# Layers' attention: sparse chunks' output products first, scaling ahead of low parts, and two output pieces' low parts formed by VectorE

## The reference, cut to what matters

```python
...
        ret = head_groupnorm(ret, g_ret[l].reshape(RET_HEADS, RET_DV).astype(jnp.float32))
        o_c = (jax.nn.silu(rg.astype(jnp.float32)) * ret.reshape(B, S, RET_HEADS * RET_DV)).astype(x.dtype)

        x = x + jnp.concatenate([o_a, o_b, o_c], axis=-1) @ w_out[l]

        hf = rmsnorm(x, g_mlp[l])
        x = x + jnp.square(jax.nn.relu(hf @ w_ff1[l])) @ w_ff2[l]
```

## Time and profile before

| | us |
|---|---|
| three runs | 1396.71, 1397.04, 1401.29 |
| median | 1397.04 |
| the profiled execution's own time | 1395.43 |
| its span | 1393.4 |
| granted TensorE clock, mean | 0.998 of full |

### The profile page before, as it was taken

One profiled execution on the slowest core, in us unless ns is written; L12 is line 12 of the kernel. 1 busy time (PEld: TensorE's weight loads), 2 busy tenths in 40 slices (PEclk: granted clock), 3 DMA queues, 4 the chain that ended last, 5 costly groups with the idle time before them and its releaser, 6 DMA issues.

```text
span 1393.4 us, 19892 instructions
## 1 busy us (share of the span) xinstructions
PE 1347.1 (97%) x7754; PEld 931.0 (67%) x7754; DVE 622.7 (45%) x1060; ACT 541.0 (39%) x790; POOL 449.3 (32%) x295
## 2 busy tenths in 40 slices
PE   8998999999999999999999999999999999999998
PEld 7786788887887788888887877755434444344343
DVE  5685554544687455353344887523202112122021
ACT  6667644435576654343555562212111111111011
POOL 2384454444374544543867913000000000000000
PEclk9999999999999999999999999999999999999999
DMA  7441454553533355455786351479999999999997
GB/s 289 137 168 67 152 181 181 185 202 127 207 116 110 116 204 190 181 182 181 237 278 225 103 208 52 137 290 411 422 428 428 427 428 428 428 427 427 428 423 292
DMA packets 50250, 351.99 MB, mean 253 GB/s; under 512 B 7747, under 2 KB 9679, under 8 KB 25583
## 3 DMA queue, kind: packets, MB, share of 16 engines
q1 hardware_dynamic: 49438, 349.52, 64.9%
q10 hardware_dynamic: 720, 1.20, 0.2%
HBM read 347.78 MB, written 1.07 MB: 250 GB/s over the span
## 4 chain that ended last, share of the span: by engine, by line
PE 72%; DMA 11%; DVE 7%; ACT 3%; issue 3%; DVEq 2%; POOL 1%; SPq 0%; ACTq 0%; POOLq 0%
PE psum L1925 12%; PE psum L1101 9%; PE psum L1103 9%; PE psum L1102 9%; PE psum L1396 9%; DMA ring<-in_w_expert_up 8%; PE psum L1946 5%; PE psum L1398 4%; PE psum L1091 4%; PE psum L1853 2%; POOL weights_split L908 1%; PE psum L1863 1%; DMA arena<-in_w_expert_down 1%; DVE arena L2577 1%; ACT weights_split L2040 1%
## 5 line engine op out<-in xcount | busy, mean ns | idle before, releaser
L908 POOL TENSOR_TENSOR weights_split<-weights_raw,weights_split 128x512 fp32r<-128x512 f32 (+2 forms) x253 | 401.6, 1621 | 338.2 <-ACT weights_split L2040 338.2
L2040 ACT ACTIVATE weights_split<-weights_raw 128x2048 fp32r<-128x2048 f32 (+4 forms) x154 | 243.5, 1586 | 243.5 <-PE psum L1103 145.3
L1925 PE MATMUL psum<-ring,arena 128*64 128x512 f32 x944 | 226.5, 598 | 12.1 <-DMA ring<-in_w_expert_up 11.2
L1396 PE MATMUL psum<-h_split,weights_split 128*128 128x512 f32 x512 | 182.1, 399 | 3.1 <-DVE h_split L2028 2.7
L1925 PEld LDWEIGHTS psum<-ring,arena 128*64 128x64 f32 x944 | 73.4, 138 | 136.4 <-issue 135.8
L1101 PE MATMUL psum<-weights_split,h_split 128*128 128x512 f32 (+3 forms) x400 | 151.9, 380 | 4.3 <-POOL weights_split L908 2.4
L1101 PE MATMUL psum<-weights_split,hidden_split 128*128 128x512 f32 (+1 forms) x384 | 151.1, 393 | 4.3 <-DVE hidden_split L2028 4.3
L908 DVE TENSOR_TENSOR weights_split<-weights_raw,weights_split 128x2048 fp32r<-128x2048 f32 (+3 forms) x53 | 119.3, 2257 | 70.1 <-ACT weights_split L2040 68.3
L1102 PE MATMUL psum<-weights_split,h_split 128*128 128x512 f32 (+3 forms) x400 | 149.5, 374 | 0.0
L1103 PE MATMUL psum<-weights_split,h_split 128*128 128x512 f32 (+3 forms) x400 | 149.2, 373 | 0.0
L1103 PE MATMUL psum<-weights_split,hidden_split 128*128 128x512 f32 (+1 forms) x384 | 147.3, 384 | 0.0
(11 more groups left out here) (379 smaller groups left out, 1734.5 us busy)
## 6 DMA issues: line engine op xcount, KB each, us to landing
weights_raw<-in_layer_w SPq DMA_DIRECT2D x94, 1024.0 KB, 4.8
arena<-in_w_expert_down SPq DMA_DIRECT2D x28, 2048.0 KB, 14.7
ring<-in_w_expert_up SPq DMA_DIRECT2D x28, 2048.0 KB, 15.0
ring<-in_w_expert_gate SPq DMA_DIRECT2D x23, 2048.0 KB, 16.2
weights_raw<-in_second_w SPq DMA_DIRECT2D x44, 512.0 KB, 4.7
arena<-in_w_expert_gate SPq DMA_DIRECT2D x4, 2048.0 KB, 10.2
ring<-in_w_expert_up SPq DMA_DIRECT2D x8, 1024.0 KB, 13.1
arena<-in_w_expert_down SPq DMA_DIRECT2D x16, 512.0 KB, 12.3
```

The lines of the kernel that those rows point to most:

```text
L908: ins = eng.tensor_tensor(W.part(j, 1, n)[:, cols], W.raw(j, n)[:, cols], W.part(j, 0, n).bitcast(F32)[:, cols], ALU.subtract)
L1396: pe.matmul(both.rearrange("p (w s) -> p w s", w=2), w[0][:, k, f * P:(f + 1) * P], hTp[:, :, k, :], start=(k == 0), stop=False)
L1925: ins = pe.matmul(bank[half(j), :], xe[h][:, k, half(j)], w[j][:, k, :], start=(k == 0), stop=(k == KD - 1))
L2040: act.activation(W.part(j, 0, w), W.raw(j, w), ACT.Copy).then_inc(W.hi, 1)
```

## The change

Five edits, all in the first block's two layers, none in what is computed:

1. TensorE: the sparse chunks (0, 1) of piece (0,1) are multiplied for both token tiles ahead of retention's chunks (2, 3): six matmuls before `turn_retained`, six after it.
2. TensorE: half of `project_out(1, 0, 0)` moves ahead of `attend_values(7)`, the other half to the end, and all of `project_out(1, 0, 1)` comes after the first `tr3` transposes. The unit `wout` 2 is finished later, after `wout` 1.
3. VectorE: `low_values(0)` comes after the rotation; from group 6 on each `norm_probs(g)` comes before the low part that stood ahead of it; `add_out(2)` comes after `add_out(1)`.
4. VectorE instead of GpSimd forms the low parts of `("out", 1, 1)` and `("out", 0, 0)`: one instruction of 2048 columns each, ahead of `norm_probs(4)` and of `norm_probs(7)`.
5. ScalarE: the high copies of pieces (0,0) and (1,0) come one group later, and `exponentials(9)` before `empty_turned(8)`.

```diff
@@ layer_plan
-    plan += [wout[0], turned[8], values[7], wout[2], turned[9], values[8], values[9], wout[1]] + turned_x[:2] + [wout[3]] + turned_x[2:]
+    plan += [wout[0], turned[8], values[7], turned[9], values[8], values[9], wout[1], wout[2]] + turned_x[:2] + [wout[3]] + turned_x[2:]
@@ layer_pieces
-    p += [(("out", c, i), "P", None if i else ("wout", T * c + T - 1)) for i in (1, 0) for c in range(2)]
+    p += [(("out", c, i), "V" if c == i else "P", None if i else ("wout", T * c + T - 1)) for i in (1, 0) for c in range(2)]
@@ TensorE
                 attend_mla(5)
+                units.wait_emptied(("O", 0))
+                project_out(0, 1, 0, (0, 1))
                 ret_ready.wait(pe, 1, l)
                 turn_retained()
-                units.wait_emptied(("O", 0), ("mixT", 3))
-                project_out(0, 1, 0, range(4))
                 units.wait_emptied(("O", 2))
-                project_out(0, 1, 1, range(4), True)
+                project_out(0, 1, 1, (0, 1))
+                units.wait_emptied(("mixT", 3))
+                project_out(0, 1, 0, (2, 3))
+                project_out(0, 1, 1, (2, 3), True)
                 turn_probs(4)
@@ 
                 turn_probs(8)
+                project_out(1, 0, 0, (0, 1))
                 attend_values(7)
-                project_out(1, 0, 0, range(4))
                 turn_probs(9)
@@ 
                 project_out(0, 0, 1, (3,))
-                project_out(1, 0, 1, (0, 1))
+                project_out(1, 0, 0, (2, 3))
                 units.wait_emptied(("wout", 0), ("wout", 1))
                 transposes(pe, units, "tr3", x, (0, 1))
-                project_out(1, 0, 1, (2, 3))
+                project_out(1, 0, 1, range(4))
@@ ScalarE
                 empty_turned(4)
-                split_after("ukv", 0, 0)
                 empty_turned(5)
                 exponentials(6)
                 high_values(4)
-                split_after("out", 0, 1)
+                split_after("ukv", 0, 0)
                 empty_turned(6)
                 exponentials(7)
                 high_values(5)
+                split_after("out", 0, 1)
                 empty_turned(7)
                 exponentials(8)
                 high_values(6)
                 split_after("out", 1, 1)
+                exponentials(9)
                 empty_turned(8)
-                exponentials(9)
@@ VectorE
                 norm_probs(3)
-                low_values(0)
                 units.wait_emptied(*(("uq", j) for j in range(2 * T)))
                 rotate(dve, *halves(q[:, :, :, NOPE:QK]), *angles(ROPE), q_tmp).then_inc(q_roped.sem, 1)
+                low_values(0)
@@ 
+                split_low(LW, dve, LW.index["out", 1, 1], l)
                 norm_probs(4)
                 norm_probs(5)
                 mask_scores(6)
+                norm_probs(6)
                 low_values(4)
-                norm_probs(6)
                 mask_scores(7)
+                split_low(LW, dve, LW.index["out", 0, 0], l)
+                norm_probs(7)
                 low_values(5)
-                norm_probs(7)
                 mask_scores(8)
+                norm_probs(8)
                 low_values(6)
-                norm_probs(8)
                 mask_scores(9)
                 add_out(0)
+                norm_probs(9)
                 low_values(7)
-                norm_probs(9)
-                add_out(2)
                 low_values(8)
                 low_values(9)
                 add_out(1)
+                add_out(2)
```

## The result

| | before | changed |
|---|---|---|
| median of the runs | 1396.88 us (4 runs, 1396.60 to 1401.29) | 1388.05 us (4 runs, 1387.26 to 1389.19) |
| the profiled execution's own time | 1395.43 us | 1389.19 us |
| its span | 1393.4 us | 1387.4 us |

The ratio is 0.9931, with a 95% interval of 0.9910 to 0.9953: 8.8 us faster, 6.6 at the least by the interval (0.47% of 1396.88). The forecast was 1390.0, in a range of 1386.5 to 1394.0.

What follows compares the result with a forecast made beforehand. TensorE was taken as the bound, with only its idles in the layers' attention to win. 2.71 + 1.0 - 0.2 = 3.5 us a layer, 7.0 in two, takes the median 1397.04 to 1390.0 us; range 1386.5 to 1394.0.

Steps and rivals of the forecast that it cites:

- The bound and what could be won: Feed-forward and expert stretches untouched; only TensorE's six idles per layer, 6.24 us, 12.5 in two layers, can be won.
- The rotation: Ahead of the transposed queries: rotation before low_values(0) starts TensorE 0.74 us earlier; 0.6 of the idle stays.
- Sparse chunks first: At retention's turn: 2.17 us idle shrinks to about 0.6; 2.15 us earlier in all by the next transpose.
- only idles count: TensorE's accounting: matmuls are the same before and after, so only idle times matter to the gain.
- VectorE's first low part: Piece (1,1) ahead of norm_probs(4): costs at most 0.35 us; total gain shrinks to 1.51 us after group 5.
- The scaling of group 6: Ahead of group 6's transpose: later copy and earlier scaling remove the whole 1.20 us; 2.71 us earlier in all.
- VectorE's second low part: Piece (0,0) ahead of group 7's scaling: in time, costs nothing; without cover 2.28 us at most.
- GpSimd and (1,0): Ahead of attend_values(7): GpSimd's remaining piece is the tightest place; 0.2 us a layer taken as loss.
- GpSimd and VectorE get in each other's way: Rival, chance 0.17: beside groups 8 and 9's scalings, 1.5 us lost a layer instead of 0.2; 1392.6 us.
- The feed-forward entry: Before ff1: twelve matmuls cover the 0.94, 0.19 grows to about 0.65, 0.41 nears 0; 1.0 us earlier.
- The sum: Whole layer: 2.71 + 1.0 - 0.2 = 3.5 us gained, 7.0 us in two layers, reaching the end.
- the contention: The 0.2 us a layer deducted for GpSimd's piece (1,0) possibly being late ahead of attend_values(7).

Runs made afterwards that it cites:

- r1: Kernel before with only low_values(0) moved behind VectorE's rotation; profiled execution 1399.76 us.
- r2: Kernel before with only TensorE's sparse chunks of piece (0,1) first for both token tiles; profiled execution 1392.46 us.
- r6: Changed kernel with ScalarE's copies of (0,0) and (1,0) back one group earlier; profiled execution 1388.57 us.
- r10: Changed kernel with low_values(4) ahead of the scaling of group 6 again; profiled execution 1387.92 us.
- r3: Changed kernel with the low parts of output pieces (1,1) and (0,0) back on GpSimd; profiled execution 1394.36 us.
- r5: Changed kernel with GpSimd's low parts in steps of 256 columns, not 512; profiled execution 1385.68 us.
- r7: Changed kernel with its second edit undone, wout 2 and add_out(2) back too; profiled execution 1387.91 us.
- r4: The changed kernel unaltered, run again beside the kernel before; median 1388.15 us against 1396.83, ratio 0.9938.
- r8: Changed kernel with ff1's first two low parts exchanged: (0,0) by VectorE, (0,1) by GpSimd; median 1385.51 us against 1396.61, ratio 0.9913.

## Why the prediction was right, and where its steps were not

**The bound and what could be won.** Right. Only idles of the attention and at the feed-forward's entry went, and the feed-forward is full in both. The expert stretch did not lengthen by what was won: from the first product on the gathered rows (L1853, L1856 after) to the end of the span it took 441.0 us in both profiles of before and 441.8 and 441.0 in those of the change. The 543 us of the rows do not show this, for they are the width of the window in both.

**The rotation.** Forecast 0.74, measured 1.0 (r1). I added the 0.42 us of `low_values(0)` to an end of 108.8 for the rotation; but VectorE's instructions follow each other 0.34 apart, not 0.42 (108.46, 108.80), the rotation began at 106.46, and TensorE started 0.05 after the end. The start is 0.14 us earlier than my 106.4 (this execution is 0.20 behind), and with the two small overlaps that makes the 0.26 us, to a few hundredths.

**Sparse chunks first.** The idle was right: 0.51 against the forecast 0.6, and retention's high part at 117.77 against 117.93. That "only idles count" was not: alone the edit took 1.76 us of idle and gave 1.2 (r2).

**VectorE's first low part.** Right in its working, and nearly in size: 119.50 to 121.78 against 119.74 to 121.94 forecast. The idle at group 4 did not show, that at group 5 was 0.23 against 0.3, from the exponentials as said. At group 6 the gain by starting times was 2.96 (132.39 to 129.43), with the changed execution 0.20 behind at the start of the stretch (107.71 and 107.91), so 3.16 against the forecast 2.71. The bracketed idles alone, 4.70 to 1.07, say 3.63: my rule that only idles count leaves out that the broken-up groups keep TensorE busy for 20.34 us and not 19.98, and a gap of 0.11 that has no bracket.

**The scaling of group 6.** Right: the whole 1.20 went. I had named two reasons, and r6 and r10 show that one of them would do. That the scaling itself would be back at 0.69 us, because GpSimd is idle beside it, I had left open ("if it again lasts 1.0 longer"); it is a third reason that no run separates.

**VectorE's second low part.** Right: hidden, its scaling at 133.7 where 133.8 was forecast. What it gained, and the first piece with it, is 0.35 us in two layers (r3).

**GpSimd and (1,0).** I took 0.2 us for a delay of the piece (1,0). That term was put in the wrong place and was too small. The piece was in time (TensorE went on at 139.60 without idle). The scaling of group 9 was not: 1.83 us, and 0.86 of idle. This is the mechanism of the rival "GpSimd and VectorE get in each other's way", at the second of its two places, and twice as large there as its 0.4. r5 shows its cause: with GpSimd's instructions half as long, the excess fell from 1.14 to 0.49. The pair of 0.69 and "1.62 and 1.72" that I had set down for the rival was a selection: the kernel before also has scalings of 0.69 (group 7, at 135.88) and 0.79 us (group 9, at 145.36) while GpSimd was at work. The rule that I set beside it (the Trainium skill, page "SBUF — State Buffer", section "SBUF: two separate sides": an exclusive lock held for the whole instruction) agrees with this, and the other direction shows too: GpSimd's piece took 7.48 us in r6, and in the kernel before its instruction at 135.92 took 1.78 us. I had priced the rule as if each meeting were TensorE's loss; the one at group 8 (1.56 us) cost TensorE nothing, since there was cover.

**The feed-forward entry, 1.0 us.** This step failed as a gain of the second edit: 1.0 us forecast, 0.23 measured (r7). The idles there went as forecast (0.94 away, 0.19 to 0.70, 0.41 away: 0.84). But taking six matmuls away from in front of group 9's transpose took away the cover of its scaling. I had worked out 0.6 us to spare there and a loss of 0.4 in the rival; it was 0.86. In idles the edit wins 0.84 and opens 0.86; the 0.23 is in the stretch without its idles.

**The sum.** 3.5 us a layer forecast. By idles 6.24 - 2.63 = 3.61 measured; by starting times the first full `ff1` stretch begins at 157.42 for 160.80, 3.38 earlier, with the 0.20 at the start 3.58. The two agree, for behind group 6 TensorE is busy for 26.42 us where it was 26.88. The total is close because the errors offset each other; that it came out at 3.6 for 3.5 is luck. By starting times it was 3.16 for 2.71 up to group 6, and behind it 0.42 for 0.8. In idles: up to group 6 it was 3.63 for 2.71, 0.92 better (0.26 at the rotation, 0.25 at retention's low part, where I counted 1.41 of the 2.17 and 1.66 went, 0.41 at groups 4 and 5, where I gave back 0.64 and 0.23 was due); the contention took 0.66 more than its 0.2; the feed-forward's entry gave 0.16 less than 1.0.

**The rest of the 8.8.** Not forecast, and only partly explained. In the two profiles of each kernel the first block's layers end 6.9 to 7.6 us earlier (x is transposed for the second block at 656.53 in both of the change, at 664.13 and 663.39 before), and the executions' own times are 5.8 to 6.8 us apart. The medians are 8.8 and 8.7 apart; over all runs here 1396.67 (36 runs) and 1388.15 (11), 8.5 apart. The executions of one kernel spread over 8 us and more (1394.37 to 1402.87 before, 1385.62 to 1394.33 after), mostly upwards. Against a forecast of 7.0 the excess of 1.5 to 1.8 us is inside this spread. The second block is no source of it that the profiles show: it is 0.8 to 1.7 us longer in those of the change (r4). One difference is on record: the mean granted clock is 0.9967 over 32 of the runs of before and 0.9977 over the 11 of the change. An estimate from these two: 0.001 of 1390 us is 1.4 us, if TensorE is the bound in all of it. That is the size of the excess, but the clocks are rounded to 0.001 and vary more than this from run to run, so the cause stays open.

## What to carry to other kernels

When an engine at 97% stands idle in a few places, list those idles one by one: each edit can be priced against its own bracket. The idles say where an edit works, the length of the stretch says what it is worth (1.76 us of idle, 1.2 us of time in r2). Matmuls moved to cover one wait uncover another: before moving filler away from a place, work out what becomes ready how late there, with the slow value of any operation that can meet a neighbour. Where VectorE must be punctual, keep GpSimd's instructions short or its work elsewhere; exchanging which engine forms which piece (r8) did more than moving work off GpSimd as such.
